# One group of level products over four PSUM banks in the linear-attention mixer of a hybrid decoder layer

## What is computed

```python
def gla_chunked(q, k, v, log_a, h0):       # q, k, log_a (B,T,H,64), v (B,T,H,128)
    def step(h, inp):
        qi, ki, vi, ai = inp
        b = jnp.cumsum(ai, axis=-2)
        diff = b[..., :, None, :] - b[..., None, :, :]
        decay = jnp.exp(jnp.where(incl[:, :, None], diff, -jnp.inf))
        attn = jnp.einsum('bhid,bhjd,bhijd->bhij', qi, ki, decay)
        o = (jnp.einsum('bhij,bhjv->bhiv', attn, vi)
             + jnp.einsum('bhid,bhdv->bhiv', qi * jnp.exp(b), h))
        ...
```

## Time and profile before

| | us |
|---|---|
| median of three runs | 3186.19 (3184.8 to 3186.38) |
| the profiled execution | 3187.0 |
| its span, first to last instruction | 3185.3 |
| TensorE matmul busy in the span | 3113.6 |
| VectorE busy | 1996.8 |
| ScalarE busy | 834.5 |
| GpSimd busy | 449.1 |

### The profile page before, as it was taken

How to read it: one execution, slowest core, us unless ns; L and a number is a source line. 1 busy time by engine, 2 the same in 40 slices (tenths; PEclk the granted TensorE clock), 3 DMA queues, 4 the chain that set the end, 5 groups by cost and what they waited for, 6 DMA issues and landing times.

```text
span 3185.3 us, 52013 instructions
## 1 busy us (share of the span) xinstructions
PE 3113.6 (98%) x20269; PEld 2019.0 (63%) x20269; DVE 1996.8 (63%) x4791; ACT 834.5 (26%) x1743; POOL 449.1 (14%) x823
## 2 busy tenths in 40 slices
PE   7999999999999999987999999999999999999998
PEld 4555555555555555544777777777766777777675
DVE  2556666666555666665466666566776666666668
ACT  2222333322332233334222211222132222212113
POOL 1000000000000000003331121111154111111110
PEclk9999999999999999997899999999999999999999
DMA  7022222222222222218411111111233111111102
GB/s 248 28 68 87 87 87 70 84 87 77 71 73 72 76 87 87 75 61 239 149 40 40 45 49 40 40 40 46 75 114 109 52 40 40 40 40 45 49 27 80
DMA packets 223169, 236.08 MB, mean 74 GB/s; under 512 B 14204, under 2 KB 167332, under 8 KB 222931
## 3 DMA queue, kind: packets, MB, share of 16 engines
q1 hardware_dynamic: 222931, 232.81, 23.3%
HBM read 203.10 MB, written 29.67 MB: 73 GB/s over the span
## 4 chain that ended last, share of the span: by engine, by line
PE 51%; DVE 0%; issue 0%; ACT 0%; DVEq 0%
PE mlp_bank L2208 34%; PE mlp_bank L2282 15%; PE mlp_bank L2296 2%; PE mlp_bank L2288 0%; DVE arena L2621 0%; DVE acc L2718 0%; ACT raw L2400 0%; DVE arena L2622 0%; PE mlp_bank L2307 0%; PE mlp_bank L2294 0%; DVE arena L2629 0%; DVE arena L2626 0%; DVE raw L2589 0%; DVE y_parts L2690 0%; DVE raw L2595 0%
## 5 line engine op out<-in xcount | busy, mean ns | idle before, releaser
L723 PE MATMUL mixer_bank<-arena,hnt 128*128 128x451 f32 x2048 | 871.0, 555 | 9.7 <-DMA arena<-in_w_in_dram 8.9
L2208 PE MATMUL mlp_bank<-arena,ws 128*128 128x256 f32 (+1 forms) x2816 | 646.1, 383 | 2.8 <-DVE raw L2595 2.8
L2208 PEld LDWEIGHTS mlp_bank<-arena,ws 128*128 128x128 f32 x2816 | 534.9, 190 | 85.6 <-DVE raw L2595 3.6
L723 PEld LDWEIGHTS mixer_bank<-arena,hnt 128*128 128x128 f32 x2048 | 364.3, 190 | 298.7 <-issue 291.4
L2282 PE MATMUL mlp_bank<-arena 128*128 128x512 f32 x1120 | 493.8, 592 | 1.0 <-DVE arena L2629 1.0
L2690 DVE TENSOR_TENSOR acc<-acc,mlp_bank 128x512 f32<-128x512 f32 x560 | 370.5, 685 | 55.7 <-PE mlp_bank L2282 55.0
L2282 PEld LDWEIGHTS mlp_bank<-arena 128*128 128x128 f32 x1120 | 212.7, 190 | 235.6 <-issue 206.2
L2657 DVE SCALAR_TENSOR_TENSOR mcv<-raw,cf,mcv 128x512 f32<-128x512 f32 (+2 forms) x352 | 262.7, 762 | 50.4 <-ACT mcv L2371 41.5
L2208 PE MATMUL mlp_bank<-arena 128*128 128x256 f32 (+1 forms) x1056 | 248.8, 386 | 5.6 <-PEq L2800 4.6
L757 PE MATMUL mixer_bank<-wo,th 128*128 128x512 f32 x512 | 246.1, 604 | 4.1 <-DMA wo<-in_w_out_dram 3.6
L2208 PE MATMUL mlp_bank<-arena,wu 128*128 128x256 f32 (+1 forms) x1056 | 246.0, 383 | 0.9 <-ACT raw L2400 0.9
(11 more groups left out here) (385 smaller groups left out, 3380.4 us busy)
## 6 DMA issues: line engine op xcount, KB each, us to landing
wo<-in_w_out_dram SPq DMA_DIRECT2D x260, 256.0 KB, 2.8
arena<-in_w_up_dram SPq DMA_DIRECT2D x44, 512.0 KB, 4.9
wu<-in_w_up_dram SPq DMA_DIRECT2D x44, 512.0 KB, 4.9
arena<-in_w_down_dram SPq DMA_DIRECT2D x40, 512.0 KB, 4.2
arena<-in_w_in_dram SPq DMA_DIRECT2D x7, 1804.0 KB, 16.6
xc<-in_x_t_dram SPq DMA_DIRECT2D x16, 512.0 KB, 4.0
xt<-in_x_prompt_dram SPq DMA_DIRECT2D x16, 512.0 KB, 5.4
xr<-in_x_prompt_dram SPq DMA_DIRECT2D x16, 512.0 KB, 3.7
```

Source lines behind the costliest of these rows:

```text
L723: x = pe.matmul(bank[ring(g)][0:N, 0:GW], hnt[:, k, 0:N], w[:, k, g * GW:(g + 1) * GW], start=(k == 0), stop=(k == KT - 1))
L2208: x = pe.matmul(out[:, 0:N], left[:, k, :], xb[:, slot, k, g * N:(g + 1) * N], start=first and k == 0, stop=k == HK - 1, skip_group_check= ...
```

## The change

All level products and the diagonal of a prompt tile are issued in one group. Levels 0 to 3 (spans 64, 32, 16, 8) go to four 128-column places of banks 5 and 7, levels 4 to 6 (spans 4, 2, 1) to three places of banks 3 and 4, and the diagonal, packed as 32 columns for each of two heads, to the last 64 columns of banks 3 and 4 (`diagonal_out`). TensorE waits once for all scaled q and k, one part of fill (part 9) goes ahead of the group, and the other parts follow it. The q transposes go to bank 5 and wait until four levels are merged; the v transposes come after `fill(20, 21)` and wait until all are merged. VectorE merges levels 0 to 3 between `conv_tap(2)` and `conv_tap(3)`, and levels 4 to 6 and the diagonal where the third set stood; the diagonal is merged in four quarters of 32 partitions for each e, eight `copy_predicated` of 64 elements a partition. The sample keeps one round in banks 5 and 7. The core of the diff:

```diff
-ROUND = 3
-ROUNDS = (NL + ROUND) // ROUND
         def level_out(a, l, e, N):
-            n = N // 2 if l < NL else N
-            c0 = 128 * (a % ROUND) if l < NL else 256
-            return bank[5 + 2 * e][0:N, c0:c0 + 2 * (64 if l < NL else 128)]\
-                .rearrange("p (g i) -> p g i", g=2)[:, :, 0:n]
+            if N == S:
+                ...
+            return bank[5 + 2 * e if a < 4 else 3 + e][:, 128 * (a % 4):128 * (a % 4) + 128]\
+                .rearrange("p (g i) -> p g i", g=2)
+
+        def diagonal_out(e):
+            return bank[3 + e][:, 3 * C:3 * C + 2 * S].rearrange("p (g i) -> p g i", g=2)
@@ TensorE
-                fill(4, 9)
-                half = (len(levels) + 1) // 2
-                pe.wait_ge(s_qe_made, 2 * t + 1)
+                fill(4, 9 if sample else 10)
+                pe.wait_ge(s_qe_made, 2 * n)
                 pe.wait_ge(s_a_abs, n)
                 pe.wait_ge(s_a_min, n)
                 for a, l in enumerate(levels + [NL]):
-                    if a % ROUND == 0:
-                        if a:
-                            fill(*((9, 12), (12, 16))[a // ROUND - 1])
-                            pe.wait_ge(s_at_level, (NL + 1) * t + a)
-                        if a <= half < a + ROUND:
-                            pe.wait_ge(s_qe_made, 2 * n)
-                        pe.sem_inc(s_held, 1)
                     for g, (keys, queries, cols), e in every(range(2), strips(l, N), range(2)):
                         ...
-                    if a % ROUND == ROUND - 1 or l == NL:
-                        x.then_inc(s_at_done, 1)
+                x.then_inc(s_at_done, 1)
                 if not sample:
-                    fill(16, 18)
+                    fill(10, 18)
+                    pe.wait_ge(s_at_level, (NL + 1) * t + 4)
                 pe.wait_ge(s_conv_silu, n)
                 for h in range(H):
-                    x = pe.transpose(heads(3)[0:N, h, :], cv[:, h, 0:N], ident[:, :])
+                    x = pe.transpose(heads(3 if sample else 5)[0:N, h, :], cv[:, h, 0:N], ident[:, :])
...
-                for h in range(H):
-                    x = pe.transpose(heads(4)[0:N, h, :], cv[:, 8 + h, 0:N], ident[:, :])
-                x.then_inc(s_v_turned, 1)
...
                 if not sample:
                     fill(20, 21)
+                    pe.wait_ge(s_at_level, (NL + 1) * n)
+                for h in range(H):
+                    x = pe.transpose(heads(4)[0:N, h, :], cv[:, 8 + h, 0:N], ident[:, :])
+                x.then_inc(s_v_turned, 1)
                 pe.wait_ge(s_q_squared, n)
@@ VectorE
-                        dve.wait_ge(s_at_done, ROUNDS * t + a // ROUND + 1)
+                        dve.wait_ge(s_at_done, n)
...
+                            else:
+                                for b in range(4):
+                                    r = slice(S * b, S * b + S)
+                                    x = dve.copy_predicated(out[r, :, r], ident[r, r].bitcast(I32).unsqueeze(1)
+                                                            .to_broadcast([S, 2, S]), diagonal_out(e)[r, :, :])
...
-                if not sample:
-                    turn_levels(0, ROUND)
                 conv_tap(2)
                 if not sample:
-                    turn_levels(ROUND, 2 * ROUND)
+                    turn_levels(0, 4)
                 conv_tap(3)
...
-                turn_levels(len(levels) if sample else 6, NL + 1)
+                turn_levels(len(levels) if sample else 4, NL + 1)
```

More of the change, by code:

```diff
@@ L401, in level_out @@
         def level_out(a, l, e, N):
-            n = N // 2 if l < NL else N
-            c0 = 128 * (a % ROUND) if l < NL else 256
-            return bank[5 + 2 * e][0:N, c0:c0 + 2 * (64 if l < NL else 128)]\
-                .rearrange("p (g i) -> p g i", g=2)[:, :, 0:n]
+            if N == S:
+                n = N // 2 if l < NL else N
+                c0 = 128 * a if l < NL else 256
+                return bank[5 + 2 * e][0:N, c0:c0 + 2 * (64 if l < NL else 128)]\
+                    .rearrange("p (g i) -> p g i", g=2)[:, :, 0:n]
+            return bank[5 + 2 * e if a < 4 else 3 + e][:, 128 * (a % 4):128 * (a % 4) + 128]\
+                .rearrange("p (g i) -> p g i", g=2)
+        def diagonal_out(e):
+            return bank[3 + e][:, 3 * C:3 * C + 2 * S].rearrange("p (g i) -> p g i", g=2)
         def strips(l, N):
@@ L838, in mixer @@
                 for a, l in enumerate(levels + [NL]):
-                    if a % ROUND == 0:
-                        if a:
-                            fill(*((9, 12), (12, 16))[a // ROUND - 1])
-                            pe.wait_ge(s_at_level, (NL + 1) * t + a)
-                        if a <= half < a + ROUND:
-                            pe.wait_ge(s_qe_made, 2 * n)
-                        pe.sem_inc(s_held, 1)
                     for g, (keys, queries, cols), e in every(range(2), strips(l, N), range(2)):
-                        out = level_out(a, l, e, N)[keys, g, cols]
                         r = slice(64 * e, 64 * e + 64)
                         if l == NL:
+                            out = level_out(a, l, e, N)[keys, g, cols] if sample else diagonal_out(e)[keys, g, :]
                             x = pe.matmul(out, qka[r, 2 + g, keys], qka[r, g, queries], start=True, stop=True)
-                        elif SPANS[l] < S:
-                            x = pe.matmul(packed(out, l), ke[r, l, g, keys], blocks(qe[r, l, g, queries], l, 1),
-                                          start=True, stop=True)
-                        else:
-                            x = pe.matmul(out, ke[r, l, g, keys], qe[r, l, g, queries], start=True, stop=True)
-                    if a % ROUND == ROUND - 1 or l == NL:
-                        x.then_inc(s_at_done, 1)
+                            continue
+                        out = level_out(a, l, e, N)[keys, g, cols]
+                        if SPANS[l] < S:
+                            pe.matmul(packed(out, l), ke[r, l, g, keys], blocks(qe[r, l, g, queries], l, 1),
+                                      start=True, stop=True)
+                        else:
+                            pe.matmul(out, ke[r, l, g, keys], qe[r, l, g, queries], start=True, stop=True)
+                x.then_inc(s_at_done, 1)
                 if not sample:
-                    fill(16, 18)
+                    fill(10, 18)
+                    pe.wait_ge(s_at_level, (NL + 1) * t + 4)
                 pe.wait_ge(s_conv_silu, n)
                 for h in range(H):
-                    x = pe.transpose(heads(3)[0:N, h, :], cv[:, h, 0:N], ident[:, :])
+                    x = pe.transpose(heads(3 if sample else 5)[0:N, h, :], cv[:, h, 0:N], ident[:, :])
                 x.then_inc(s_q_turned, 1)
@@ L1255, in mixer @@
                     .then_inc(s_a_ln, 1)
-                act.wait_ge(s_at_done, ROUNDS * t)
+                act.wait_ge(s_at_done, t)
                 act.wait_ge(s_qe_made, 2 * t)
@@ L1313, in mixer @@
                 act.wait_ge(s_q_turned, n)
-                act.activation(qsq[0:N, :, :], heads(3)[0:N, :, :], ACT.Square).then_inc(s_q_squared, 1)
+                act.activation(qsq[0:N, :, :], heads(3 if sample else 5)[0:N, :, :], ACT.Square).then_inc(s_q_squared, 1)
                 act.wait_ge(s_kl_turned, n)
@@ L1526, in turn_levels @@
                         for e in range(2):
-                            out, new = at[0:N, e, :, 0:N], level_out(a, l, e, N)
+                            out = at[0:N, e, :, 0:N]
+                            new = level_out(a, l, e, N) if l < NL or sample else None
                             if l < NL:
@@ L1532, in turn_levels @@
                                                         packed(new, l))
-                            else:
+                            elif sample:
                                 msk = ident[0:N, 0:N].bitcast(I32).unsqueeze(1)
                                 x = dve.copy_predicated(out, msk.to_broadcast([N, 2, N]), new)
+                            else:
[3 more added lines that the diff above has]
+                                                            .to_broadcast([S, 2, S]), diagonal_out(e)[r, :, :])
                         x.then_inc(s_at_level, 1)
```

## The result

The changed kernel takes 3231.28 us (four runs, 3230.79 to 3234.38) against 3186.28 us in the same comparison, a ratio of 1.014 with an interval of 1.0127 to 1.0153. It is 45 us slower where 10 us faster was forecast. Its profiled span is 3229.5 us.

A forecast was written before the change was run, and what follows sets the result against it. TensorE, busy 3113.6 of 3185.3 us, was taken as the bound in tiles 1 to 14. 14 x (0.61 - 0.05) + 2 x 1.1 = 10.0 us gained, giving a median of 3176.2 us, range 3171.5 to 3181.4.

The forecast's parts named there:

- the sum for TensorE: Level products of each tile: one group takes 2.34 us in place of 2.95 in three rounds, gaining 0.61 us.
- What 32 records cost inside a group: Middle strips of the level products on TensorE: 0.27 us for 32 records, read from round 2's 96 in 0.92 us.
- What moves behind it, at no cost: Work after the group in each tile: later steps all covered, with 1.0 us to spare at the v transposes.
- a wait on VectorE's merges: Before the v transposes in tiles 1 to 14: none expected; one there would prove the forecast wrong.
- The diagonal's eight pieces: VectorE's last merges: 0.18 us a piece, 1.4 us in all, with bounds of 0.1 and 0.30 us each.
- rival 2: Last merges stall TensorE at the v transposes if diagonal pieces exceed 0.28 us; 3200 us at 0.5 each; chance 0.05.
- Tiles 0 and 15: First and last prompt tiles, not bound by TensorE: third tap earlier, gaining 1.1 us each, bounds 0 and 1.3.
- The gain of one group in itself: Tiles 1 to 14: 0.61 us less 0.05 for the new wait, a period shorter by 0.56 us.
- The wait for all scaled q and k: Before the group on TensorE: charged 0.05 us a tile, bounds 0 and 0.15, with no cover.
- rival 3: End of the mixer: half-rate clock spells may shift, about 1.7 us either way; no chance of its own.
- the 25 ns of the rule: Level strips on TensorE: about 60 cycles per matmul, 6 us a tile for 256; the forecast followed the trace instead.
- the high end: Slow end of the whole-kernel range, 3181.4 us: longer wait, less from tiles 0 and 15, adverse clock, half an edge kept.

The follow-up runs named there:

- e3: The kernel before the change with round 2's matmuls issued three times over, 288 records in a row into the same two banks; 3280.25 us, one run.
- e4: The changed kernel with all levels and the diagonal written into banks 5 and 7 only, so scores are not the reference's; 3233.75 us, one run.
- e6: The changed kernel with six levels merged between the taps in place of four; 3219.55 us, ratio 1.0102.
- e9: The changed kernel with six levels merged early and levels in strips of 64 keys, 272 instructions a group in place of 448; 3180.09 us, ratio 0.9983.
- e7: The changed kernel with its group split in two, three parts between, a signal after each, six levels merged early; 3184.85 us, ratio 0.9995.
- e5: The changed kernel with each level of a prompt tile as four whole-level matmuls in place of strips; 3212.18 us, ratio 1.0078.

## Why the prediction was wrong

**The step that failed** is the sum for TensorE: "What 32 records cost inside a group" was taken from 96 records in a row and carried on to 224. The rate held as long as there were instructions: 2.12 us in tile 4. But 224 records with their weight loads are 448 instructions in 2.1 us, and 256 of them take 3.45 us or a little more to come (e3). A group of 96 records can't hold 256 instructions; one of 224 holds a whole block of them wherever its first block border falls within its first 192 instructions, which is in three places of four. The forecast counted matmuls and never instructions. The profile of before could have raised the question: its page lists the instruction queue, and 161 packets are as many as TensorE's instructions make in blocks of about 250.

A halt costs 2.1 to 2.7 us. Behind most of them TensorE's granted clock falls to 0.50, and four wide matmuls take up to 1.8 us more (tile 3); behind those of tiles 1 and 11 it stays at 1.00. Tiles 2, 3, 5, 6, 8, 9, 13 and 14 lose 4.0 us each on average, tiles 1, 11 and 15 together 8.5 us.

Which tiles are spared follows from where the blocks of 256 begin. TensorE has 1698 instructions a tile (835 matmul and 835 weight-load records and 28 waits and the like of its sequencer), 162 more than six blocks. So a border comes 94 instructions, 47 records, later in each tile. The halts do just that: in tiles 2, 3, 5, 6, 8, 9, 11, 13 and 14 they come after 143, 190, 156, 203, 169, 216, 182, 148 and 195 records of the group. From tile to tile the place moves on by 47, less 128 where that leads past the group's 224. In the spared tiles 4, 7, 10 and 12 the same count gives 109, 122, 135 and 101: too little of the group stands before the border to hold a whole block, or in tile 10 hardly more than one. At 122 and 135 e4 and e6 have halts of under 0.9 us.

**"What moves behind it, at no cost"** was wrong at the v transposes, where the time at which VectorE ends was mis-sized in three places. The prediction had named a wait on VectorE's merges there as a sign that would prove it wrong. VectorE in tile 4 of the changed kernel, against the earlier trace rows:

```profile
453.33 0.69 DVE L1488 TENSOR_TENSOR yo<-mixer_bank,xr 128x512 f32<-128x512 f32 x1 [0.93 <-PE mixer_bank L762]
454.82 1.90 DVE L1658 SCALAR_TENSOR_TENSOR cv<-th,cv 128x512 f32<-128x512 f32 x3 [0.79 <-ACT th L1306]
...
459.06 2.20 DVE L1530 COPY_PREDICATED at<-level,mixer_bank 128x128 f32<-128x128 int32 x6
461.39 1.89 DVE L1539 COPY_PREDICATED at<-ident,mixer_bank 32x64 f32<-32x64 int32 x8
463.31 0.69 DVE L1686 TENSOR_REDUCE qss<-th 128x4 f32<-128x512 f32 x1
```

Counted from the start of part 8 (439.30), the SiLU starts at 15.5 us, forecast 14.8. ScalarE's tanh waits not only for the third tap but also for the last part of the output projection, whose stationary operand lies in the tile that it overwrites; before, that part was done first and the wait could not be seen:

```profile
453.30 1.48 ACT L1306 ACTIVATE th<-cv 128x1536 f32<-128x1536 f32 x1 [12.93 <-PE mixer_bank L762]
```

The three levels take 2.33 us to the start of the diagonal, 0.3 more than in the sum. The diagonal's eight pieces take 0.24 us each, forecast 0.18. The advice to keep the count of operations low, which the prediction takes from the section on the DRAIN, stands in the Trainium skill, "VectorE: DVE Perf Modes", Rules for kernel authors. The pieces came out between the 0.18 of the sum and its bound of 0.30. The end comes at 24.0 us where 22.5 was forecast; TensorE's arrival, 23.5, was right. So 0.57 us a tile are lost, which takes the whole gain of a tile: hence 88.1 us in the tiles without a halt. This is rival 2's place, but it alone would have given no change (e6 and tile 4), and slower was given 0.05 for it. It also came at 0.24 us a piece, below the 0.28 that the rival asked for, since the other two places took the cover away.

**Tiles 0 and 15** were given 1.1 us each and gave nothing. In tile 0 the first half held: the q transposes come at 95.40 us, forecast 95.2, before 96.27, in spite of a halt of 1.6 us. Then TensorE waits for the diagonal, and the k transposes come at 102.36, before 101.97:

```profile
101.87 0.66 PE L905 MATMUL mixer_bank<-ident,cv 128*128 128x128 f32 x4 [1.08 <-DVE at L1539]
```

In tile 15 it waits 0.83 us for the last scaled q and k, halts for 1.94 and waits 2.94 us for the diagonal. The halts are not the whole reason, since without them nothing is gained there either: in e9 tile 0's k transposes are at 103.59, and tile 15's period is 87.30 against 87.09.

**What held.** The gain of one group in itself: 0.56 us a tile was forecast, and the period is 87.45 to 87.65 us in the tiles of e6 without a halt and 87.41 in e9, against 88.1. The wait for all scaled q and k cost nothing that shows in tiles 1 to 14. Two groups gave half (e7). The q transposes never waited in those tiles. The clock, rival 3, was seen too narrowly: it was thought of for the end of the mixer, where the half-rate spell of e7 took back most of 2 us, and not as what follows a halt.

**Slips in the working**, of no weight for the outcome. A tile has 224 matmul records in the levels and the diagonal, not 256, so by the 25 ns of the rule they would cost 5.6 us. The terms of the high end add up to 4.8 us and not 5.2 (1.4 for the wait, 1 for tiles 0 and 15, 1.7 for the clock, 0.7 for half an edge), so the range would end at 3181.0.

**Open.** How many instructions are held ahead and when the next block is asked for was not tried by itself. In tile 3 the halt ends some 2.4 to 2.7 us after the packet's start (351.9 to 352.2 against 354.63), and the packets of a halted tile start 3.4 to 4.0 us apart; what fills that time stays open. So does why the clock fell behind most halts and not behind those of tiles 1 and 11. Why tile 0 comes later in e7 and e9 was not tried either.

## What to carry to other kernels

Count the instructions of a run of small matmuls, weight loads included, and the time in which TensorE uses up 256 of them. By the 3.45 us of e3, an estimate for other kernels, a time clearly below that can end in a halt, and the clock can add most of 2 us to it. Put wide matmuls between such runs, or cover the same work with fewer and larger tiles of the array. When a step is moved, look for each wait that was met before and hence not seen, and size it from the code, not from the old timeline.

## What the runs showed of the hardware

- TensorE's stream halts for want of instructions without a named releaser, mostly for 1.3 to 2.9 us, where 256 of them come with no wide matmul among them (changed kernel, e3, e4, e6). Where a tile has two halts, they are 128 matmul records with their weight loads apart (e3).
- Behind most halts of 2.0 to 2.7 us the granted clock is 0.50: in tile 3, four wide matmuls take 3.50 us in place of 1.71. Behind the halts of tiles 1 and 11, of 2.0 and 2.6 us, it is 1.00.
- A level of 64-row matmuls costs 0.27 us in 32-key strips and about 0.25 us in 64-key strips (104 records in 1.76 us), but 0.47 us with weights of 128 columns (e5).
